# The first mixer's attention scores kept per chunk of 64 tokens instead of per tile of 128

## The reference, cut to what matters

```python
def step(S, inp):
    q_c, k_c, v_c, a_c = inp
    b = jnp.cumsum(a_c, axis=-2)
    diff = b[..., :, None, :] - b[..., None, :, :]
    dec = jnp.exp(jnp.where(causal, diff, -jnp.inf))
    attn = jnp.einsum('bhid,bhjd,bhijd->bhij', q_c, k_c, dec)
    o = (jnp.einsum('bhid,bhde->bhie', q_c * jnp.exp(b), S)
         + jnp.einsum('bhij,bhje->bhie', attn, v_c))
    b_last = b[..., -1:, :]
    S = (jnp.exp(b_last)[..., 0, :, None] * S
         + jnp.einsum('bhjd,bhje->bhde', k_c * jnp.exp(b_last - b), v_c))
    return S, o
```

## Time and profile before

| | |
|---|---|
| Time, median of 3 runs | 2805.38 us (2793.61 to 2810.98) |
| Profiled execution: its own time | 2807.38 us |
| Profiled execution: its span | 2805.6 us |
| Mean granted TensorE clock | 0.951 of 2.4 GHz |
| Busy share of the span | PE 94%, DVE 39%, ACT 24%, POOL 9% |
| The stage of the change, gla | about 390 to 567 us of the span |

### The profile page before, as it was taken

How to read it: one execution, slowest core, us unless ns; L and a number is a source line. 1 busy time by engine, 2 the same in 40 slices (tenths; PEclk the granted TensorE clock), 3 DMA queues, 4 the chain that set the end, 5 groups by cost and what they waited for, 6 DMA issues and landing times. The chain is left out here.

```text
span 2805.6 us, 48229 instructions
## 1 busy us (share of the span) xinstructions
PE 2629.8 (94%) x18983; PEld 2409.6 (86%) x18984; DVE 1093.2 (39%) x1937; ACT 659.4 (24%) x1341; POOL 251.3 (9%) x222
## 2 busy tenths in 40 slices
PE   5999977869989889999999999999999999999798
PEld 4887756649855689999999999999999999999666
DVE  3367629462422352222322323323232323232365
ACT  3224333255311101111111111111111111111245
POOL 0000114035210000000000000000000000000120
PEclk9999976589999789999999999999999999999899
DMA  3111220000053166667888888999999999998541
GB/s 120 54 52 50 86 68 1 23 1 1 16 174 127 62 197 213 222 226 246 257 269 267 274 283 276 304 290 299 291 305 299 302 300 303 301 302 284 201 171 68
DMA packets 439487, 531.87 MB, mean 190 GB/s; under 512 B 12148, under 2 KB 407240, under 8 KB 439368
## 3 DMA queue, kind: packets, MB, share of 16 engines
q1 hardware_dynamic: 425448, 481.08, 52.3%
q0 software_dynamic: 13920, 49.03, 5.6%
HBM read 489.44 MB, written 40.63 MB: 189 GB/s over the span
## 5 line engine op out<-in xcount | busy, mean ns | idle before, releaser
L1590 PE MATMUL ex_psum<-ex_xT,weight_ring_a 128*128 128x134 f32 (+14 forms) x6144 | 768.5, 286 | 0.8 <-ACT ex_xT L1576 0.8
L1590 PEld LDWEIGHTS ex_psum<-ex_xT,weight_ring_a 128*128 128x128 f32 x6144 | 758.7, 191 | 1.2 <-issue 1.2
L1630 PE MATMUL ex_psum<-ex_hT,weight_ring_b 128*128 128x134 f32 (+14 forms) x4096 | 521.5, 286 | 0.0
L1630 PEld LDWEIGHTS ex_psum<-ex_hT,weight_ring_b 128*128 128x128 f32 x4096 | 508.1, 191 | 0.0
L1600 DVE TENSOR_SCALAR ex_gate<-ex_psum,bias_gate_up 128x192 f32<-128x192 f32 x256 | 95.0, 413 | 693.8 <-PE ex_psum L1590 678.5
L1590 PE MATMUL ex_psum<-ex_xT,weight_ring_b 128*128 128x134 f32 (+14 forms) x2048 | 255.6, 286 | 0.0
L1590 PEld LDWEIGHTS ex_psum<-ex_xT,weight_ring_b 128*128 128x128 f32 x2048 | 252.2, 191 | 0.0
L1604 DVE TENSOR_SCALAR ex_up<-ex_psum,bias_gate_up 128x192 f32<-128x192 f32 x256 | 95.0, 413 | 400.9 <-PE ex_psum L1590 400.9
L1617 ACT ACTIVATE ex_sig<-ex_gate 128x384 f32<-128x384 f32 x128 | 66.9, 523 | 718.3 <-DVE ex_gate L1600 718.0
L1638 ACT ACTIVATE ex_yT<-ex_psum,bias_down 128x192 f32<-128x192 f32 x256 | 93.6, 417 | 533.4 <-PE ex_psum L1630 533.4
L1896 PE MATMUL project_psum<-n_hi,w_in_hi 128*128 128x512 f32 x464 | 187.4, 404 | 5.1 <-DVE n_lo L397 5.1
(11 more groups left out here) (320 smaller groups left out, 3070.5 us busy)
## 6 DMA issues: line engine op xcount, KB each, us to landing
weight_ring_a<-in_w_gate_up SPq DMA_DIRECT2D x192, 1024.0 KB, 6.0
weight_ring_b<-in_w_down SPq DMA_DIRECT2D x128, 1024.0 KB, 6.3
weight_ring_b<-in_w_gate_up SPq DMA_DIRECT2D x64, 1024.0 KB, 5.1
y_dram<-ex_y_a SPq DMA_DIRECT2D x33, 512.0 KB, 3.4
w_in_pieces<-in_w_in SPq DMA_DIRECT2D x29, 512.0 KB, 3.2
y_dram<-ex_y_b SPq DMA_DIRECT2D x33, 256.0 KB, 3.7
project_work<-in_x SPq DMA_DIRECT2D x8, 512.0 KB, 3.4
gates_dram<-project_work POOLq DMA_DIRECT2D x16, 256.0 KB, 2.7
```

The source lines that it names most:

```text
L1590: mm = pe.matmul(self.ps[:, bank, i * CAP:i * CAP + width], w[:, k, i * P:(i + 1) * P], self.xT[:, k, 0:width], start=(k == 0), stop=(k == ...
L1630: mm = pe.matmul(self.ps[:, bank, i * CAP:i * CAP + width], w[:, k, i * P:(i + 1) * P], self.hT[:, k, 0:width], start=(k == 0 and i == 0), ...
```

## The change

- The scores `A` become [P, NH, NT, C]: of each tile only the two 64x64 blocks on the diagonal, chunk 2t on partitions 0 to 63 and chunk 2t+1 on 64 to 127. The masks are cut to that form on DVE (`cut`, four copies).
- A step makes its scores per chunk: 32 products of 64 rows, 64 columns of weights and 64 moving columns, in place of 16 of 64, 128 and 128. They fill two PSUM banks a step, so four steps fit, and `keep` is 2 COPY_PREDICATED of 512 elements in place of 4.
- The distance is made only where it is used: DVE `q_distance` for the second halves, POOL `k_distance` for the first halves, each 512 elements, with signs such that no Abs is needed; ACT does one Exp of 1024 elements a step in place of Abs and Exp. The products with queries (DVE) and keys (POOL) are half as long as well. `Q` is cleared on DVE and `K` on POOL before that, as half of each is not written.
- In the output phase the product with the scores is two of 64 rows and 64 output partitions in place of one of 128 and 128; the state products stay as they are, and the order is scores(r=0), state(r=0), scores(r=1), state(r=1).

```diff
         w_gate = sb("w_gla_gate", [16, 2 * P])
         b = sb("gla_b", [P, 2, T])
-        A = sb("gla_scores", [P, NH, NT, P])
+        A = sb("gla_scores", [P, NH, NT, C])
+        cut = sb("gla_level_masks", [P, 1 + LEVELS, C])
         dist = sb("gla_dist", [P, 2, T])
         Q = sb("gla_q_level", [P, 2, T])
         K = sb("gla_k_level", [P, 2, T])
...
-        def bank_of(step, half, parity):
-            return 4 * (step % 2) + 2 * half + parity
+        def bank_of(step, parity):
+            return 2 * (step % 4) + parity
+        def halves(ap, level):
+            m = 1 << level
+            v = ap.rearrange("p (a i) -> p a i", i=2 * m)
+            return v[:, :, 0:m], v[:, :, m:2 * m]
+        def middle(level, p):
+            m = 1 << level
+            return b[:, p, :].rearrange("p (a i) -> p a i", i=2 * m)[:, :, m - 1:m].to_broadcast([P, T // (2 * m), m])
         @block.sync
         def _(sp):
...
             pool.memset(A[:], 0.0).then_inc(zeroed, 1)
             pool.memset(qe[:], 0.0).then_inc(zeroed, 1)
             pool.memset(S[:, :, 0, :], 0.0).then_inc(zeroed, 1)
+            pool.wait_ge(run_sum, 2)
+            pool.memset(K[:], 0.0).then_inc(zeroed, 1)
+            def k_distance(n):
+                level, p = STEPS[n]
+                if n >= 4:
+                    pool.wait_ge(q_done, n - 3)
+                    pool.wait_ge(k_done, n - 3)
+                pool.tensor_tensor(halves(dist[:, n % 2, :], level)[0], middle(level, p), halves(b[:, p, :], level)[0], ALU.subtract).then_inc(k_dist, 1)
+            k_distance(2)
+            k_distance(3)
             for n in range(2, len(STEPS)):
                 level, p = STEPS[n]
                 pool.wait_ge(decay_done, n - 1)
                 if n >= 4:
-                    pool.wait_ge(score_done, 4 * (n - 1))
-                pool.tensor_tensor(K[:, n % 2, :], g.gqkT[:, 2 + p, :], dist[:, n % 2, :], ALU.mult).then_inc(k_done, 1)
+                    pool.wait_ge(score_done, 2 * (n - 1))
+                else:
+                    pool.wait_ge(zeroed, 5)
+                pool.tensor_tensor(halves(K[:, n % 2, :], level)[0], halves(g.gqkT[:, 2 + p, :], level)[0], halves(dist[:, n % 2, :], level)[0],
+                                   ALU.mult).then_inc(k_done, 1)
+                if n + 2 < len(STEPS):
+                    k_distance(n + 2)
...
                     pe.wait_ge(q_done, n - 1)
                     pe.wait_ge(k_done, n - 1)
-                    pe.wait_ge(kept, 4 * (n - 1))
-                for half in range(2):
-                    for parity in range(2):
-                        rows = slice(GK * parity, GK * (parity + 1))
-                        for i in range(4):
-                            t = 4 * half + i
-                            cols = slice(t * P, (t + 1) * P)
-                            kk, qq = (g.gqkT[rows, 2 + p, cols], g.gqkT[rows, p, cols]) if level == "diag" else (K[rows, n % 2, cols], Q[rows, n % 2, cols])
-                            mm = pe.matmul(ps[:, bank_of(n, half, parity), i * P:(i + 1) * P], kk, qq, start=True, stop=True)
-                        mm.then_inc(score_done, 1)
+                if n >= 4:
+                    pe.wait_ge(kept, 2 * (n - 3))
+                for parity in range(2):
+                    rows = slice(GK * parity, GK * (parity + 1))
+                    for c in range(NC):
+                        t, r = c // 2, c % 2
+                        cols = slice(c * C, (c + 1) * C)
+                        kk, qq = (g.gqkT[rows, 2 + p, cols], g.gqkT[rows, p, cols]) if level == "diag" else (K[rows, n % 2, cols], Q[rows, n % 2, cols])
+                        mm = pe.matmul(ps[C * r:C * (r + 1), bank_of(n, parity), t * C:(t + 1) * C], kk, qq, start=True, stop=True)
+                    mm.then_inc(score_done, 1)
             for q in range(4):
                 p, half = q // 2, q % 2
                 pe.wait_ge(kd_done, p + 1)
-                pe.wait_ge(kept, 4 * len(STEPS))
+                pe.wait_ge(kept, 2 * len(STEPS))
...
                 for h in range(NH):
-                    pe.matmul(ps[:, bank, h * P:(h + 1) * P], A[:, h, t, :], g.gv[:, t, h * P:(h + 1) * P],
-                              start=(h == 0), stop=False, skip_group_check=True)
                     for r in range(2):
+                        rows = slice(C * r, C * (r + 1))
+                        pe.matmul(ps[rows, bank, h * P:(h + 1) * P], A[rows, h, t, :], g.gv[rows, t, h * P:(h + 1) * P],
+                                  start=(h == 0), stop=False, skip_group_check=True)
                         mm = pe.matmul(ps[C * r:C * (r + 1), bank, h * P:(h + 1) * P], qe[:, h, t * P + C * r:t * P + C * (r + 1)],
                                        S[:, h // 2, 2 * t + r, :], start=False, stop=(h == NH - 1), skip_group_check=True)
                 mm.then_inc(out_done, 1)
...
             for n in range(2, len(STEPS)):
-                act.wait_ge(dist_done, n - 1)
-                act.activation(dist[:, n % 2, :], dist[:, n % 2, :], ACT.Abs).then_inc(edge_exp, 1)
-                act.wait_ge(edge_exp, n - 1)
-                act.activation(dist[:, n % 2, :], dist[:, n % 2, :], ACT.Exp, scale=-1.0 / 16).then_inc(decay_done, 1)
+                act.wait_ge(q_dist, n - 1)
+                act.wait_ge(k_dist, n - 1)
+                act.activation(dist[:, n % 2, :], dist[:, n % 2, :], ACT.Exp, scale=1.0 / 16).then_inc(decay_done, 1)
...
             dve.wait_ge(run_sum, 2)
-            dve.wait_ge(zeroed, 3)
-            def distance(n):
+            def q_distance(n):
                 level, p = STEPS[n]
-                m = 1 << level
-                v = b[:, p, :].rearrange("p (a i) -> p a i", i=2 * m)
                 if n >= 4:
                     dve.wait_ge(q_done, n - 3)
                     dve.wait_ge(k_done, n - 3)
-                dve.tensor_tensor(dist[:, n % 2, :].rearrange("p (a i) -> p a i", i=2 * m), v,
-                                  v[:, :, m - 1:m].to_broadcast([P, T // (2 * m), 2 * m]), ALU.subtract).then_inc(dist_done, 1)
+                dve.tensor_tensor(halves(dist[:, n % 2, :], level)[1], halves(b[:, p, :], level)[1], middle(level, p), ALU.subtract).then_inc(q_dist, 1)
             def q_level(n):
                 level, p = STEPS[n]
                 dve.wait_ge(decay_done, n - 1)
                 if n >= 4:
-                    dve.wait_ge(score_done, 4 * (n - 1))
-                dve.tensor_tensor(Q[:, n % 2, :], g.gqkT[:, p, :], dist[:, n % 2, :], ALU.mult).then_inc(q_done, 1)
+                    dve.wait_ge(score_done, 2 * (n - 1))
+                dve.tensor_tensor(halves(Q[:, n % 2, :], level)[1], halves(g.gqkT[:, p, :], level)[1], halves(dist[:, n % 2, :], level)[1],
+                                  ALU.mult).then_inc(q_done, 1)
             def keep(n):
                 level, p = STEPS[n]
-                mask = g.k[:, K_ID:K_ID + P] if level == "diag" else g.k[:, K_LEVEL + level * P:K_LEVEL + (level + 1) * P]
-                for half in range(2):
-                    for parity in range(2):
-                        dve.wait_ge(score_done, 4 * n + 2 * half + parity + 1)
-                        dve.copy_predicated(A[:, 2 * p + parity, 4 * half:4 * half + 4, :],
-                                            mask.bitcast(I32).unsqueeze(1).to_broadcast([P, 4, P]),
-                                            ps[:, bank_of(n, half, parity), :].rearrange("p (t c) -> p t c", t=4)).then_inc(kept, 1)
-            distance(2)
-            distance(3)
+                mask = cut[:, 0 if level == "diag" else 1 + level, :]
+                for parity in range(2):
+                    dve.wait_ge(score_done, 2 * n + parity + 1)
+                    dve.copy_predicated(A[:, 2 * p + parity], mask.bitcast(I32).unsqueeze(1).to_broadcast([P, NT, C]),
+                                        ps[:, bank_of(n, parity), :].rearrange("p (t c) -> p t c", t=NT)).then_inc(kept, 1)
+            q_distance(2)
+            q_distance(3)
+            for r in range(2):
+                rows, cols = slice(C * r, C * (r + 1)), slice(C * r, C * (r + 1))
+                dve.tensor_copy(cut[rows, 0, :], g.k[rows, K_ID:K_ID + P][:, cols]).then_inc(masks_done, 1)
+                dve.tensor_copy(cut[rows, 1:, :], g.k[rows, K_LEVEL:K_LEVEL + LEVELS * P].rearrange("p (l c) -> p l c", c=P)[:, :, cols]).then_inc(masks_done, 1)
+            dve.memset(Q[:], 0.0).then_inc(zeroed, 1)
+            dve.wait_ge(masks_done, 4)
+            dve.wait_ge(zeroed, 5)
             for n in range(len(STEPS)):
                 keep(n)
                 if n + 2 < len(STEPS):
                     q_level(n + 2)
                 if n + 4 < len(STEPS):
-                    distance(n + 4)
+                    q_distance(n + 4)
...
```

(7 more changed lines are left out.)

## The result

The changed kernel takes 2817.38 us, median of 13 runs (2814.97 to 2819.28), the one before 2796.53 in as many (2793.34 to 2813.62): a ratio of 1.0062, 95% interval 1.0047 to 1.0077. It is slower by 13 to 22 us (the medians are 21 apart); the forecast was faster by 6. The 13 times of the kernel before lie in two groups, near 2795 and near 2808 us, and both traces of it (2807.4 and 2807.9 us) are of the upper one.

The account below looks back on a forecast made before the run. DVE was taken to bound the levels and PE the output phase. 17 us gained and 11 lost leave 6, from the median of 2805.38 a forecast of 2799 us (chance 0.5), range 2778 to 2818.

Parts of the forecast that it names:

- 17 gained: Levels of gla: a step of 4.0 us in place of 5.55, last copies done at 474.9 against 491.87 us.
- 11 lost: Output phase on PE: 0.34 us more a head, over 32 heads, counted in full as PE is the bound.
- sum of a head in the output phase: PE, output phase: four changes of shape at 0.275 us plus eight records, 1.69 us a head against 1.35 before.
- 0.065 and 0.083 for a record: PE, output phase: assumed us for each record, 0.065 for the 64x64 scores and 0.083 for the states.
- The count of changes: PE, output phase: four changes of shape a head instead of two; by the skill's rule their count decides and the phase slows.
- the small tiles overlap: Rival, output phase: score pairs run beside state products, 5 us gained there and 20 in the levels, 2780 us; chance 0.17.
- The upper bound: PE, output phase: 0.36 us per change of shape, 2.03 us a head, 22 us lost.
- The rival that ended slower: Output phase eats the levels' gain: 22 us lost on PE between scores and states, 14.6 gained, 2813 us; chance 0.2.
- The levels: POOL and DVE exclude each other, 3.65 to 3.8 us a step; PE 3.0 to 4.2; 4.0 taken, 17 us gained.
- every operation 1.6: Rival, levels: short runs cost POOL 1.6 us or more an operation, gain 11.6 or less, 2805 us, no change; chance 0.13.
- Level 0: Levels, operands with every second element: nothing to 1.3 us more; by the skill about 2 us less gain.
- The clock: PE clock in the levels: 4.2 us a step if at 0.50, 3.65 if at 1.0; shifts the forecast by 3 us or so.

Follow-up runs that it names:

- Head groups: Changed kernel with, for each head of the output phase, both score products first and then both state products: 2769.30 us in one run.
- halves apart: Changed kernel, a tile's scores before its states, each with all heads of r=0 and then all of r=1: 2761.70 us, ratio 0.9874 to the kernel before.
- other half: Changed kernel with each head's output-phase order scores 0, state 1, scores 1, state 0: 2813.58 us in one run.
- one shape: Kernel before with its score product split into two of 128 rows and 64 output partitions, the state products' shape: 2781.54 us, ratio 0.9930.
- tile groups: Changed kernel with the 8 score products of a tile first, then its 8 state products: 2755.71 us, ratio 0.9837 to the kernel before.

## Why the prediction was wrong

The sign was wrong, and by one kind of term. 17 gained less 11 lost was forecast, 24 less 37 was found.

- *The failed step* is the sum of a head in the output phase, "4 x 0.275 + 4 x 0.065 + 4 x 0.083 = 1.69". The change of shape wasn't the error. It brought 0.62 - 0.27 = 0.35 us from a group's last start to the next group, that is 0.27 more than the 0.083 in which I had counted a start, as forecast. (Against a record at 0.21 a change costs some 0.2, so it isn't dearer than forecast by that count either, and 4 x (2 x 0.21 + 0.2) = 2.48 is what a head takes.) What was wrong is 0.065 and 0.083 for a record. Both come from rows in which products on different parts of PE run beside each other: for 0.083 the two column halves take turns, and for 0.065, read record by record, four products start within 0.04 us of each other and the next four 0.21 later. A record that has its column half to itself costs 0.21; the rows of the transposes had it, at 0.233 on average. With one product alone on one half between two changes, its second record starts 0.27 us after the first. Two records then cost what four did: 0.62 us. I took a mean over overlapping work for the price of one piece of it, and the change is what takes the overlap away. 4 x 0.62 = 2.47, 0.78 more a head than forecast, 25 us for 32 heads: that is the miss of the phase (37 against 11), but for 1 us in the transposes, which now stand before a change too (1.05 to the next start, 0.91 before). Head groups show it (four records at 0.62), halves apart once more.
- *The count of changes* as the mechanism was right, and so was the rule of the Trainium skill that spoke against the change (TensorEngine Tiling (Array Packing), section Tiling Modes: a change of the tiling mode drains the engine). By it the phase had to get slower, and it did; other half and one shape agree with it (0.62 us a group with changes, 0.43 without). That the small tiles overlap in this order was a rival at 5 us gained; it is refuted by the 2.47 us a head.
- *The upper bound* of that phase, 22 us, was none: it varied the price of a change and left the 0.065 and 0.083 fixed. The rival that ended slower, at 2813, with the chance 0.2, had the right place, but made the change of shape dear (0.36) where the records were. It had 22 lost and 14.6 gained, where the traces show 37 and 24.
- *The range* held by luck: 2817 lies in 2778 to 2818 since both were built on 2805.4, the median of three runs, and 13 runs of the same kernel gave 2796.5. Built on that, the range would end at 2809, the forecast would be 2790 and the slower rival 2804.
- *The levels* were read rightly, with the size off. DVE's 2.5 us of own work and the exclusion of POOL and DVE were as forecast. The step is 3.41 in place of 4.0: PE ran at the lower end, 0.048, not near 0.065, and POOL's distance takes 0.9, under the 1.04 of its nearest row, as it starts while DVE has the right (the key product takes 1.12 behind such a wait and 1.27 without). The shared right needs 3.4 where I had 3.65. Short runs cost POOL 0.25 us in each of four key products (1.51 to 1.53 in place of 1.27); they didn't make every operation 1.6. The first level product stood at 425.05, forecast 425.6.
- *Level 0.* The trace shows two DVE distances with every second element in 1.29 us (417.24), the pitch of all others. By the Trainium skill (Vector Engine (DVE) Microarchitecture Reference, section Measured stream behaviour on trn2), 1.75 ns or more an element, they would take 0.9 us or more each, an estimate from the page's figure for 512 elements. For a step of two elements the measurement says otherwise, and it decides.
- *The clock.* It fell to 0.50 in the levels (0.67 before), as allowed for, and stayed at 0.50 in the output phase in both kernels.
- *Open:* gla is 13 us longer in the profiled executions, the medians are 21 us apart. The executions of the kernel before near 2795 us have the higher mean clock; in which stage isn't seen, as none of them has a trace. Nor is it settled why the clock rises in one order and not in the other.

## What to carry to other kernels

When products of two tile shapes alternate on PE, sort them by shape: the same products were 62 us faster in the changed kernel with the tile's scores first and its states behind, which at 2755.7 us beats the kernel before by 1.6%. A pace that is read from rows in which pieces overlap is a price only while the overlap stays; ask what the new order does to the neighbours before using it. Smaller products that bring changes of shape may cost PE more than the full one that they replace: 2.47 us a head with the states here, in place of 1.35.

## What the runs showed of the hardware

- At the lower clock, a group of 64x64 or 128x64 products between two changes of shape takes 0.62 us with two records as with four.
- PE was busy for 87 of 90 us in the changed output phase and its clock stayed at 0.50 of 2.4 GHz; with the same products grouped, or all of one shape, it was at 0.90 and 0.91. The kernel before had the same in 51 us at 0.50. With tile groups the order alone accounts for most of the gain. At the lower clock a tile would take 4.8 to 5.2 us against 10.9, by an estimate: a group of eight pairs 0.27 + 6 x 0.21 + 0.35 = 1.9 (the one measured at that clock took 2.26), twice, and 1.05 for the transposes. That is 46 to 49 of the 62 us; the clock brings the tile to 2.63.
- POOL's two-input operation of 512 elements took 1.27 us with runs of 4 elements and more, 1.51 to 1.53 with runs of 1 and 2, and 0.9 with one operand repeated, its wait for DVE taken off. Behind such a wait it is some 0.15 us shorter than when it starts free (1.12 against 1.27).
- Read record by record, the level products start in pairs on the two column halves, 0.006 us apart, and a pair every 0.107 us at the lower clock: neighbours on different halves run as one.
